# Adding the band mask to attention scores: four bfloat16 products a pair on PE, or four VectorE adds in PSUM

## What is computed

```python
def attend(qb, k, v, mask=None, sink=None):
    scale = qb.shape[-1] ** -0.5
    s = jnp.einsum('bqkgd,bskd->bkgqs', qb, k).astype(jnp.float32) * scale
    if mask is not None:
        s = jnp.where(mask, s, -jnp.inf)
    m = jnp.max(s, axis=-1, keepdims=True)
    if sink is not None:
        sk = sink.astype(jnp.float32)[None, :, :, None, None]
        m = jnp.maximum(m, sk)
        e = jnp.exp(s - m)
        denom = jnp.sum(e, axis=-1, keepdims=True) + jnp.exp(sk - m)
    ...
    p = (e / denom).astype(v.dtype)
    return jnp.einsum('bkgqs,bskd->bqkgd', p, v)
```

## Time and profile before

| | |
|---|---|
| median of 3 runs | 1530.26 us (1529.27 to 1533.38) |
| the profiled execution | 1539.47 us, of which the span is 1537.7 us |
| granted PE clock, mean | 0.964 |
| PE busy | 1399.2 us, 91% of the span |
| PE weight loads busy | 844.3 us, 55% |
| DVE busy | 624.9 us, 41% |
| ACT busy | 346.7 us, 23% |
| POOL busy | 233.2 us, 15% |

### The profile page before, as it was taken

The page is one execution under the profiler, slowest core; times in us unless marked ns, Lnnn a source line. Parts: engine busy times, 40 slices in busy tenths (PEclk is TensorE's granted clock), DMA queues, the critical chain, the costliest instruction groups (busy, mean ns, idle before and its releaser), DMA issues.

```text
span 1537.7 us, 25812 instructions
## 1 busy us (share of the span) xinstructions
PE 1399.2 (91%) x10352; PEld 844.3 (55%) x10352; DVE 624.9 (41%) x1450; ACT 346.7 (23%) x933; POOL 233.2 (15%) x295
## 2 busy tenths in 40 slices
PE   4999998998998998898989999988989999969985
PEld 1876685332776686333664456853327766854332
DVE  0136625433456525242522343254334247252435
ACT  1105512110214612110210343121102036121101
POOL 0100022111122022110200000221112000212103
PEclk9999999999999999999989999999999999979998
DMA  9998138999978238999857502489999880238994
GB/s 332 331 313 278 73 107 325 386 420 414 331 284 238 83 131 295 386 416 420 321 212 248 118 29 96 162 328 381 420 414 340 286 307 2 82 124 299 421 422 166
DMA packets 121633, 412.96 MB, mean 269 GB/s; under 512 B 13531, under 2 KB 55486, under 8 KB 96934
## 3 DMA queue, kind: packets, MB, share of 16 engines
q1 hardware_dynamic: 95686, 346.13, 59.6%
q0 software_dynamic: 18880, 61.23, 12.2%
q10 hardware_dynamic: 6944, 3.91, 0.8%
HBM read 387.12 MB, written 26.66 MB: 269 GB/s over the span
## 4 chain that ended last, share of the span: by engine, by line
PE 73%; DMA 8%; DVE 8%; issue 4%; ACT 3%; POOL 1%; SPq 1%; DVEq 0%; POOLq 0%; ACTq 0%
PE bank L1867 65%; PE bank L2037 3%; ACT pp L1165 2%; PE bank L2202 2%; DMA y_slots<-kT 2%; DMA V<-in_swa_wqkv 1%; DMA ids<-own_id,row_of 1%; DVE x L1297 1%; DMA hT<-h_rows,id_of 1%; PE bank L1922 1%; DMA xn<-y_slots,row_of 1%; DMA id_of<-ids 1%; DVE hT L1289 1%; SPq L689 1%; PE bank L2214 1%
## 5 line engine op out<-in xcount | busy, mean ns | idle before, releaser
L1867 PE MATMUL bank<-ring,pp 128*32 128x512 f32 x2112 | 342.9, 606 | 17.4 <-issue 13.4
L1867 PE MATMUL bank<-ring,hT 128*128 128x256 f32 (+3 forms) x998 | 233.3, 392 | 5.3 <-DVE hT L1289 2.7
L1867 PEld LDWEIGHTS bank<-ring,hT 128*128 128x128 f32 x998 | 181.3, 191 | 54.2 <-issue 26.8
L1867 PE MATMUL bank<-work,pp 128*32 128x512 f32 x704 | 176.1, 609 | 8.6 <-DVE kT L1735 5.1
L1867 PEld LDWEIGHTS bank<-ring,pp 128*32 128x32 f32 x2112 | 92.5, 111 | 157.5 <-issue 155.7
L1867 PE MATMUL bank<-ring,xn 128*128 128x256 f32 x768 | 168.2, 380 | 0.0
L1867 PEld LDWEIGHTS bank<-ring,xn 128*128 128x128 f32 x768 | 145.0, 190 | 19.4
L1867 PE MATMUL bank<-V,pp 128*32 128x512 f32 x480 | 114.0, 629 | 5.3 <-issue 4.7
L1165 ACT ACTIVATE pp<-bank,neg_max 128x384 f32<-128x384 f32 x192 | 96.7, 525 | 13.3 <-DVE neg_max L1631 10.1
L1743 DVE TENSOR_TENSOR pp<-bank,pp 128x256 f32<-128x256 f32 x36 | 15.3, 425 | 198.0 <-ACT pp L1235 198.0
L910 POOL TENSOR_TENSOR x<-x,pp 128x256 f32<-128x256 f32 x48 | 38.3, 799 | 371.0 <-DVE pp L1704 371.0
(11 more groups left out here) (279 smaller groups left out, 1793.3 us busy)
## 6 DMA issues: line engine op xcount, KB each, us to landing
ring<-in_w_mod SPq DMA_DIRECT2D x70, 1024.0 KB, 8.2
ring<-in_moe_w_gate SPq DMA_DIRECT2D x40, 1024.0 KB
ring<-in_moe_w_up SPq DMA_DIRECT2D x40, 1024.0 KB, 15.6
ring<-in_moe_w_down SPq DMA_DIRECT2D x36, 1024.0 KB
gbc<-in_w_mod SPq DMA_DIRECT2D x17, 1024.0 KB, 11.8
work<-in_moe_w_down SPq DMA_DIRECT2D x16, 1024.0 KB, 15.2
y_slots<-kT POOLq DMA_DIRECT2D x28, 512.0 KB, 8.6
work<-in_moe_w_gate SPq DMA_DIRECT2D x12, 1024.0 KB
```

The costliest lines, as they stand in the source:

```text
L1867: return pe.matmul(out, lhsT, rhs, start=start, stop=stop)
```

## The change

The products of mask and unit matrix are gone from PE, and with them the bfloat16 copies, their two casts, the semaphore and PE's wait for it. Instead DVE adds the float32 triangle to the 128 columns in the bank, just ahead of the head's first reduce, and waits for that add's end before it reduces.

```diff
@@ -361,8 +361,6 @@
-        ident_h = ctx.enter_context(nc.sbuf_tensor("ident_h", [P, P], BF16))
-        masks_h = ctx.enter_context(nc.sbuf_tensor("masks_h", [P, 2, P], BF16))
@@ -487,8 +485,8 @@
-        lat_sq, lat_rstd, states, wr_ready, first_ready, masks_ready = (sem(s) for s in
-            ("lat_sq", "lat_rstd", "states", "wr_ready", "first_ready", "masks_ready"))
+        lat_sq, lat_rstd, states, wr_ready, first_ready = (sem(s) for s in
+            ("lat_sq", "lat_rstd", "states", "wr_ready", "first_ready"))
@@ -1540,9 +1538,7 @@
                     dve.wait_ge(const_in, 16 * 18)
-                    V_.tensor_copy(ident_h[:, :], ident[:, :])
                     V_.tensor_copy(own_id[:, :], beyond[:, 0:NB])
-                    V_.tensor_copy(masks_h[:, :, :], masks[:, :, :]).then_inc(masks_ready, 1)
@@ -1627,6 +1623,9 @@
                         wait_bank_full(dve, key)
+                        if kind == 0:
+                            banded = job_bank(key)[:, P * (1 - half):P * (2 - half)]
+                            link(V_.tensor_tensor(banded, banded, masks[:, half, :], ALU.add))
                         for b, c0, w in PARTS[half]:
@@ -2016,12 +2015,7 @@
                         ins = mm(job_bank(key)[:, 0:384], qT[r, q, b * P:(b + 1) * P], kT[r, kk, P:4 * P],
-                                 True, kind != 0)
-                        if half == 1 and kind != 0:
-                            done(ins)
-                    for key in keys if kind == 0 else ():
-                        ins = mm(job_bank(key)[:, P * (1 - half):P * (2 - half)], ident_h[:, :], masks_h[:, half, :],
-                                 False, True)
+                                 True, True)
                         if half == 1:
                             done(ins)
@@ -2117,9 +2111,6 @@
-                    if L == 0:
-                        pe.wait_ge(const_in, 16 * 18)
-                        pe.wait_ge(masks_ready, 1)
```

## The result

| | before | changed |
|---|---|---|
| median of 7 runs each, us | 1533.38 (1529.27 to 1538.19) | 1545.33 (1538.19 to 1551.40) |
| ratio | 1 | 1.0068, 95% interval 1.0049 to 1.0088 |
| profiled execution, us (span) | 1539.47 (1537.7) | 1549.38 (1547.6) |

The ratio is that of the mean times. The change makes the kernel slower by 7.5 to 13.5 us. The forecast of +6.4 us is a ratio of 1.0042, on the right side and a little under the interval. In the forecast's own terms, 1.0068 × 1530.26 = 1540.7 us stands against 1536.7 and lies in its range of 1530 to 1544. The median of 1545.33 itself lies above that range; the median of before has moved too, from 1530.26 with three runs to 1533.38 with seven.

The account below looks back on a forecast made before the run. PE bounded the kernel at 6.73 us a pair; four adds make the DVE and ACT loop 7.14. Layer 0's 3.6 plus layer 3's 2.8 gives +6.4 us on 1530.26, so 1536.7, range 1530 to 1544.

Parts of the forecast that it names:

- PE at 6.73 with products, 6.25 without: Windowed attention: PE needs 6.73 us a pair of heads with mask products, 6.25 without, a difference of 0.48.
- The loop of 5.82 us through DVE and ACT: Windowed attention: time from one turn-copy start to the next through DVE and ACT, without adds and nothing waiting for PE.
- 0.91 us shorter than PE's 6.73: Windowed attention: slack of the 5.82 us DVE and ACT loop against PE's period before the change.
- The rival of a pure gain: Windowed attention: DVE's slack swallows adds costing under 0.11 us each; 7.7 us gained, 1522.6 us; chance 0.06.
- c = 0.33, from the 256- and 384-element rows: DVE in layers 0 and 3: each add costs 0.33 us, 0.30 duration plus 0.03 wait; bounds 0.31 and 0.435.
- the first rival: DVE adds overlap their neighbours: 0.22 us each, period 6.70, no change, 1530.5 us; chance 0.17.
- PE idle 0.9 us a pair for the probabilities: Layer 0's middle pairs: PE waits some 0.9 us a pair for ACT's probabilities, as DVE and ACT set the pace.
- Layer 0, 56.12 us forecast: Layer 0, first reduce to last reciprocal: 52.48 us becomes 56.12, eight periods of 7.14 less 0.58 and 0.42; +3.6.
- the clock rival: PE's clock falls in layer 0 as in layer 3: 3.3 us on top, 1540; chance 0.07 including 0.01 for a lasting fall.
- Layer 3, +2.8 forecast: Layer 3's attention: PE's low clock hides the adds of the first two pairs, 0.8 us, leaving +2.8 of 3.6.
- The rest moves as a block: Outside the two attentions: nothing later takes time back, since loads wait for free buffers; effect nothing.

Follow-up runs that it names:

- e5: Changed kernel with ACT's two sink exponentials issued ahead of its first turn-copy; 1542.72 us, ratio 1.0023 to before.
- e11: Kernel before with ACT's two sink exponentials issued ahead of its first turn-copy; one execution, 1542.05 us.
- e10: Changed kernel with every DVE mask add done twice, each with its wait; one execution, 1570.45 us.
- e7: Kernel before with half 0's mask by DVE add, half 1's by PE product, sink exponentials ahead of ACT's copy; 1535.96 us, ratio 0.9991.
- e4: Kernel before with DVE adds in layer 0 only, PE mask products kept in layer 3; 1543.72 us, ratio 1.0026.
- e8: Changed kernel measured once more, unaltered; 1544.91 us, ratio 1.0048 to before.
- e1: Changed kernel with the two unused bfloat16 tiles still allocated, so later tiles keep their place; 1546.50 us, ratio 1.0043 to before.
- e6: Kernel before with the mask product last in each half and half 0's context scores ahead of the 384 columns; 1533.62 us, ratio 0.9970.
- e3: Changed kernel without the add, so no mask at all in layers 0 and 3; 1530.79 us, ratio 0.9941 to before.

## Why the prediction held, and where it was off

- **PE at 6.73 with products, 6.25 without**: held. The kernel without a mask runs at 6.24.
- **The loop of 5.82 us through DVE and ACT:** held, as the loop that four adds make the longest. 7.09 − 4 × 0.33 = 5.77. The copy's hop was 0.43 and not 0.47, the two sink exponentials 0.49 and not 0.54. That it is this loop which decides is shown from both sides: the same step on ACT gives 0.48 where the loop paces (e5) and nothing where PE does (e11), and four more adds cost their full 1.33 us (e10).
- **"0.91 us shorter than PE's 6.73":** wrong, by a second path that the sum left out. ACT takes up half 1's exponentials only when it is through with half 0's. Two rows of the kernel before, from the pair of the earlier trace rows, the end of half 0's maxima and the second head's exponential:

```profile
142.81 0.23 DVE L1636 TENSOR_SCALAR neg_max<-neg_max,sink 128x2 f32<-128x2 f32 x1
143.32 0.59 ACT L1165 ACTIVATE pp<-bank,neg_max 128x384 f32<-128x384 f32 x1
```

  From the copy at 140.64 to 143.04 are 2.40 us; the hop to ACT 0.03; from 143.32 ACT works without a pause to the end of the sink exponentials at 146.71, 3.39; then 0.10 + 0.20 + 0.11 as in the forecast. That is 6.23 us without any add, and e7 gives the same: 6.42 − 2 × 0.33 + 0.47 = 6.23. The slack to PE was 0.50 us on this path and only 0.02 against PE's 6.25. It did not spoil the forecast, since only half 0's two adds lie on it: 6.23 + 2 × 0.33 = 6.89, under the other path's 7.09. The first path was summed rightly; that the one left out stayed shorter was luck. The rival of a pure gain had less room than its c under 0.11.
- **c = 0.33, from the 256- and 384-element rows**: held. 0.29 for the add and 0.03 to 0.04 for the wait, 0.33 from start to start, and the next four cost as much (e10). Written back to PSUM, the add took what the rows that write to SBUF give when carried down to 128 elements; no run has the same add with SBUF as its output.
- **The 0.22 of the first rival:** it does not follow from the rule that the prediction takes from the Trainium skill (VectorE: DVE Perf Modes, section The DRAIN you can't avoid). If the pipe empties whether or not there is a wait, an add costs at least its whole 0.30. As a mechanism of its own it is excluded by the period.
- **PE idle 0.9 us a pair for the probabilities:** 0.60 in the one wait of a pair. From 141.92 to 149.01 PE was busy 6.49 us and not the 6.25 that I gave it; that is the rest. DVE's wait for the sinks was 0.60 and not 0.7.
- **Layer 0, 56.12 us forecast, 56.45 and 57.31 measured:** the middle was 0.05 a period shorter than I had it. The first pair was longer, by 0.36 and 1.44 us over the 7.09. That is the clock rival in part: I gave it 3.3 us and a chance of 0.06, and it came in seven of the nine profiles with adds in layer 0. So the sum for this layer is near the measured 56.45 partly by luck: a middle read too long hides part of a fall of the clock that I had left out. The fall cost less than 3.3, I take it because a PE at half speed hides in part under the slower loop of DVE and ACT. No run isolates that, but two fit it: layer 3 took 0.68 us more than layer 0 in e10, whose loop of 8.42 leaves PE room (clock 0.64 over 8 us), and 3.30 more in before, where PE has none (0.57).
- **Layer 3, +2.8 forecast:** this is the step that failed. I took its low clock for a property of the kernel before and let it hide part of the adds. It does not come with the layer's instructions: the same ones took 53.90 us in e4 (clock 0.79), and in e11, with only ACT's sink exponentials moved, 52.01 (clock 1.00). The profile pair shows +0.4 because the clock fell less after the change. Against 53.90 the adds cost 2.3 and 2.9 (56.17 and 56.78). Against a layer 3 at full clock they cost 3.7 and 4.3, taking that as layer 0's 52.48 (e11's two layers differ by 0.05).
- **"The rest moves as a block":** too bold for a single pair of profiles. Outside the attentions before took 1295.0 and 1298.2 us, the changed kernel 1300.5 and 1293.9. In a profile pair this noise is as large as the effect. The slices of DMA traffic that I cited as after both attentions lie in part inside them: they cover 153.8 to 230.7 and 1268.6 to 1345.5 us, and the attentions end at 183.9 and 1311.9.

The sum: the attentions of layers 0 and 3 together take 112.6 and 114.1 us in the changed kernel, 108.3 and 108.0 in the two profiles of before, 106.4 if layer 3 goes as it went in e4, and 105.0 if it keeps its full clock as in e11. That makes 4.4 to 9.1 us; the timed runs say 7.5 to 13.5, 4.6 to 10.1 (e8) and 4.2 to 9.1 (e1), which overlap from 7.5 to 9.1. The attentions can account for all of that, if most timed executions of before have a milder layer 3 than its two profiles. That is not shown, since the timed runs have only a mean clock for the whole execution. Their clocks do say that part of the loss goes with a lower one: among runs at 0.966 to 0.971, five of e8 stand 6.1 us above 24 of before, and seven of e1 4.8 above 16 of before, near the forecast of 6.4, while all of their runs stand 8.0 and 6.6 above in the mean. A fall of the clock in layer 0's first pair is itself part of that.

The rivals: that the adds overlap (period 6.70) and that DVE's slack swallows them (6.25) are both excluded by the period of 7.09, in both profiles of the changed kernel. The clock did not fall in the middle pairs.

**Still open:** what makes the clock fall in one execution and not in the next, and why e5's runs had it low so often; why e7's time stayed above what its attentions say; and whether the waits for gathered rows follow in any way from when a layer's attention ends.

## What to carry to other kernels

Idle time of an engine is not slack of its loop: add up the loop that runs through it, and compare it with the busiest engine's period before moving work there. There can be more than one such loop through the same engines, and each has a slack of its own. Here 1.37 us of idle time in a pair held 0.91 of slack on one path and 0.50 on the other, and the adds of 0.33, four on the first and two on the second, were too many for both. And before taking a cheap operation off the engine that sets the pace, look at where it stands there: half 0's two products cost 0.42 us a pair in their old place and 0.08 in the new order, and that reordering gained time where exchanging products for adds lost it.

## What the runs showed that I had not expected

- **The order counts more than the product.** The mask products of the first half cost PE 0.42 us between two kinds of scores that use 64 rows each (1.49 + 0.48 against 1.07 + 0.48 without them), and 0.08 as the last of the half, with the two kinds side by side (1.29 + 0.34). Whether it is the product's place or the new order of the scores is not separated. Those of the second half, always last, cost 0.07: 1.06 + 0.34 in e6 against 0.85 + 0.48 in e3.
- **The clock of a stage's first pair is not a property of the kernel.** In layer 0 it was 1.00 in the four profiles with products alone (before twice, e6, e11), and below it in seven of the nine with adds there, and in e3 with neither; e7 and e10, with pauses as long, kept it. Of the changed kernel itself one execution had 0.85 and one 0.50, at 0.36 and 1.44 us. The Trainium skill (TensorE: Matmul & The Clock Gate, section Part 1: The HAM clock gate) also says, of the warm-up at a kernel's start, that one kernel's slow matmuls differ in number from run to run; these first pairs vary likewise from one execution to the next.
